# The combining pass beside the last two expert blocks, with their rows made up in two gathered tiles

## The reference, cut to what matters

```python
out = lax.map(expert_block, (blk_expert, buf_tok.reshape(n_blocks, MOE_BLOCK)))
out = out.reshape(n_rows, D_MODEL) * buf_w[:, None]
y = jax.ops.segment_sum(out, buf_tok, num_segments=n_tok + 1)[:n_tok]
...
h = h + hier_moe(...)          # residual
y_prompt = rms_norm(yp, norm_final_w)
y_sample = rms_norm(ys, norm_final_w)
```

## Time and profile before

| | |
|---|---|
| median of 3 runs | 1506.51 us |
| profiled execution's own time | 1505.11 us |
| its span | 1503.4 us |
| PE, DVE, ACT, POOL busy | 1416.1, 1061.5, 766.1, 568.4 us |
| mean rate of the DMA engines | 240 GB/s, 361.07 MB |

### The profile page before, as it was taken

The page is one execution under the profiler, slowest core; times in us unless marked ns, Lnnn a source line. Parts: engine busy times, 40 slices in busy tenths (PEclk is TensorE's granted clock), DMA queues, the critical chain, the costliest instruction groups (busy, mean ns, idle before and its releaser), DMA issues. The chain is left out here.

```text
span 1503.4 us, 21686 instructions
## 1 busy us (share of the span) xinstructions
PE 1416.1 (94%) x7625; PEld 1233.0 (82%) x7625; DVE 1061.5 (71%) x1225; ACT 766.1 (51%) x891; POOL 568.4 (38%) x345
## 2 busy tenths in 40 slices
PE   6999999999999999899999659999999999999976
PEld 5999999999999998788877548888888888888852
DVE  6687722366666664545463579999999999999956
ACT  6332222333333335344433438777777777777734
POOL 2323324454444442485644014333433333333311
PEclk9999999999999999999999669999999999999997
DMA  5222333234444445876653659999999999999958
GB/s 197 65 78 86 126 95 111 80 130 143 144 141 147 138 144 167 294 219 239 209 168 130 231 201 383 402 396 390 377 381 362 389 379 383 385 388 387 369 211 343
DMA packets 115793, 361.07 MB, mean 240 GB/s; under 512 B 18772, under 2 KB 48468, under 8 KB 99348
## 3 DMA queue, kind: packets, MB, share of 16 engines
q1 hardware_dynamic: 100164, 322.37, 58.6%
q0 software_dynamic: 15568, 37.87, 7.3%
HBM read 316.52 MB, written 59.64 MB: 250 GB/s over the span
## 5 line engine op out<-in xcount | busy, mean ns | idle before, releaser
L2048 DVE TENSOR_TENSOR wgu_l<-wgu,wgu_h 128x2048 fp32r<-128x2048 f32 x128 | 290.0, 2288 | 27.4 <-ACT wgu_h L1928 26.5
L1928 ACT CAST wgu_h<-wgu 128x2048 fp32r<-128x2048 f32 x124 | 237.4, 1915 | 100.6 <-PE bank0and L64 100.5
L62 PE MATMUL bank0and<-wgu_h,xh_blk 128*128 128x512 f32 x512 | 203.7, 398 | 2.9 <-DVE xl_blk L2052 2.9
L64 PE MATMUL bank0and<-wgu_h,xl_blk 128*128 128x512 f32 x512 | 200.9, 392 | 0.0
L62 PE MATMUL bank0and<-xh,wh 128*128 128x352 f32 x576 | 197.6, 343 | 3.0 <-ACT raw L906 3.0
L63 PE MATMUL bank0and<-wgu_l,xh_blk 128*128 128x512 f32 x512 | 200.3, 391 | 0.0
L64 PE MATMUL bank0and<-xh,wl 128*128 128x352 f32 x576 | 186.7, 324 | 0.0
L63 PE MATMUL bank0and<-xl,wh 128*128 128x352 f32 x576 | 186.5, 324 | 0.0
L1671 POOL TENSOR_TENSOR wol<-wo,woh 128x1024 fp32r<-128x1024 f32 x48 | 121.4, 2536 | 123.5 <-ACT woh L996 123.5
L1835 POOL DMA_INDIRECT scratch_picked<-yb,dst x31 | 92.7, 2991 | 197.5 <-DVE yb L2042 197.5
L2057 DVE TENSOR_TENSOR wd_l<-wd,wd_h 128x1024 fp32r<-128x1024 f32 x128 | 148.2, 1219 | 1.2 <-ACT wd_h L1934 1.0
(11 more groups left out here) (496 smaller groups left out, 3234.5 us busy)
## 6 DMA issues: line engine op xcount, KB each, us to landing
wgu<-in_w_gate_up SPq DMA_DIRECT2D x128, 1024.0 KB, 7.6
wd<-in_w_down SPq DMA_DIRECT2D x128, 512.0 KB, 7.6
wo<-in_w_out SPq DMA_DIRECT2D x48, 512.0 KB, 4.9
w<-in_w_in_tiles SPq DMA_DIRECT2D x36, 512.0 KB, 3.6
yy<-scratch_picked SPq DMA_DIRECT2D x8, 1024.0 KB, 12.6
scratch_xb<-stage POOLq DMA_DIRECT2D x10, 512.0 KB, 4.0
xb<-scratch_xb SPq DMA_DIRECT2D x8, 640.0 KB, 4.4
scratch_uT<-feat SPq DMA_DIRECT2D x8, 528.0 KB, 5.0
```

The source lines that it names most:

```text
L62: nc.tensor.matmul(acc, lh, rh, start=start, stop=False)
L64: return nc.tensor.matmul(acc, ll, rh, start=False, stop=stop)
L1928: nc.scalar.copy(wgu_h[:, s], wgu[:, s]).then_inc(gu_high, 1)
L2048: nc.vector.tensor_tensor(wgu_l[:, s], wgu[:, s], wgu_h[:, s].bitcast(F32), ALU.subtract).then_inc(gu_split, 1)
```

## The change

`combine` is gone as a function and as a stage; its work is written at the end of each engine's program in `experts`. Order of the parts:

- At the start of `experts` SP writes the gates to DRAM (`gates`, T x 2), and loads `w_final` and the residual tiles 0 to 3 right after the weights of block 1, instead of after the last down load. Residual tiles 8 and 4 now go ahead of the last block's down weights, 5 to 7 behind them.
- POOL zeroes `yb` and scatters it twice, to the rows of `picked` that belong to the last two blocks.
- SP begins to load `yy` when the scatter of block 29 has landed (m*16+32 counts the two extra scatters and blocks 0 to 29) and the part of `wgu_h` that a tile overwrites has been used.
- DVE makes the list `out_row`: the token's number, or out of bounds where one of its two copies is in one of the last two blocks. The output of tiles 0 to 8 goes through indirect stores with this list into one output `y` (T rows).
- POOL scatters blocks 30 and 31 only after every `yy` tile has been loaded, block 31 after block 30 has landed. Then it gathers by the token lists of these two blocks the residual rows, gates and picked rows into two extra tiles, 9 and 10, which are summed, normalised and stored like the others. The store of tile 10 waits for all stores before it.
- PE sums tiles 2, 4, 6, 7; DVE sums 8, 1, 0, 3, 5, 9, 10.

```diff
@@ SP
+            for t in range(2):
+                rows, n = ((slice(0, SEQ), P), (slice(SEQ, T), TS))[t]
+                tiles = slice(0, NT) if t == 0 else slice(NT, NT + 1)
+                sp.dma_start(S["gates"][rows, :].rearrange("(t p) k -> p t k", p=n), S["gate"][0:n, tiles, :]).then_inc(loaded[0], 16)
             m = blocks_but_three(sp) + 1
             load_gate_up(1)
+            sp.wait_ge(rows_ready, 1)
+            sp.dma_start(w_final[:], A["norm_final_w"][0].partition_broadcast(P)).then_inc(loaded[0], 16)
+            for t in range(FIRST):
+                sp.dma_start(h[t], S["h"][t * P:t * P + P, :]).then_inc(loaded[t], 16)
             with sp.Fori(0, m) as i:
                 load_gate_up(i + 2)
                 load_down(i + 1)
+            sp.wait_ge(gu_split, m * 4 + 8)
+            load_h(NT)
+            load_h(4)
             load_down(m + 1)
+            for t in (5, 6, 7):
+                load_h(t)
             sp.wait_ge(y_stored, m * 16 + 32)
+            for t in (8, 1, 0, 2, 3, 4, 5, 6, 7):
+                used = 0 if t == 0 else (t + 1) // 2
+                if used:
+                    sp.wait_ge(gu_used, m * 4 + (4 + used))
+                sp.dma_start(yy[t][0:live(t)], picked[t * P:t * P + live(t)]).then_inc(loaded[t], 16)
@@ POOL
             gather(1)
+            for j in range(2):
+                if j:
+                    pool.wait_ge(y_stored, 16)
+                then_own(pool, nc.gpsimd.tensor_copy(dst[:], of_row[:, 1, bass.ds(m + (1 + j), 1)]), dst_ready, j + 1)
+                pool.indirect_dma_start(out=S["picked"], out_offset=bass.IndirectOffsetOnAxis(ap=dst[:], axis=0),
+                                        in_=yb[:], in_offset=None, bounds_check=2 * T - 1, oob_is_err=False).then_inc(y_stored, 16)
             gather(2)
...
             scatter(m)
+            is_loaded(pool, 0)
+            def store(n):
+                t = ORDER[n]
+                rows = out_row[0:r, t:t + 1] if t <= NT else late_row[:, t - NT - 1, 0:1]
+                pool.wait_ge(out_ready, n + 2)
+                pool.indirect_dma_start(out=A["y"], out_offset=bass.IndirectOffsetOnAxis(ap=rows, axis=0), in_=h[t][0:r, :], ...)
+            late_gather(0, h[NT + 1], S["h"])
+            for j in range(2):
+                late_gather(j, late_gate[:, j, :], S["gates"])
+            for n in range(STORED_FIRST):        # 2
+                store(n)
+            for t in range(NT + 1):
+                is_loaded(pool, t)
             scatter(m + 1)
...                                              # scatter of block 31, after block 30 has landed
+            for n in range(STORED_FIRST, STORED_FIRST + 2):
+                store(n)
+            pool.wait_ge(down_split, m * 4 + 12)
+            pool.wait_ge(y_stored, m * 16 + 80)
+            for k in range(2):
+                late_gather(0, yy[NT + 1][:, k, :], S["picked"], k)
+            late_gather(1, h[NT + 2], S["h"], 0, xg_loaded)
+            for k in range(2):
+                late_gather(1, yy[NT + 2][:, k, :], S["picked"], k, xg_loaded)
+            for n in range(STORED_FIRST + 2, NT + 2):
+                store(n)
+            pool.wait_ge(out_stored, 16 * (NT + 2))
+            store(NT + 2)
@@ DVE, after the loop
+            ...                                  # out_row, four small instructions
+            make_diag(0)
+            make_diag(1)
             gated(m + 1)
             low_down(m + 1, range(2))
             low_hid(m + 1, (last_h, last_l))
+            make_diag(2)
+            make_diag(3)
             unload_y(m)
             low_down(m + 1, range(2, 4))
+            add(NT)
             dve.wait_ge(down_used, (m + 1) * 4 + 4)
             nc.vector.tensor_copy(xg[:], S["banks45"][:]).then_inc(y_done, 1)
+            add(1); norm(NT); add(0); norm(1); norm(0); add(3); norm(2); norm(3); add(5)
+            norm(4); norm(5); norm(6); add(9); norm(7); norm(9)
+            dve.wait_ge(xg_loaded, m * 16 + 80)
+            add(10); norm(10)
```

More of the change, by code:

```diff
@@ L1918, in _ @@
             down(m + 1, first=4)
+            for n, t in enumerate(ON_PE):
+                is_loaded(pe, t)
+                if n == 0:
+                    pe.wait_ge(diag_ready, 8)
+                    pe.wait_ge(hT_done, m + 2)
+                if n >= 2:
+                    pe.wait_ge(y_done, m + (n - 1))
+                for half in range(2):
+                    s = slice(half * 512, (half + 1) * 512)
+                    acc = psum_of(t, half)
+                    nc.tensor.matmul(acc, C["ident"][:], h[t][:, s], start=True, stop=False)
+                    nc.tensor.matmul(acc, diag[n // 2][:, n % 2, 0, :], yy[t][:, 0, s], start=False, stop=False)
+                    nc.tensor.matmul(acc, diag[n // 2][:, n % 2, 1, :], yy[t][:, 1, s], start=False, stop=True).then_inc(pe_summed, 1)
         @block.scalar
@@ L2204, in norm @@
                                                          op0=ALU.mult, op1=ALU.mult)
                 ins.then_inc(out_ready, 1)
[L2207 to L2209 removed]
+            flat_last = in_last[:].rearrange("p t k -> p (t k)")
+            after(nc.vector.tensor_scalar(flat_last, of_block[:], 2.0, blk_end[:, E - 1:E], ALU.add, ALU.is_ge))
@@ new lines, in _ @@
+            after(nc.vector.tensor_reduce(out_row_f[:], in_last[:], AX.X, ALU.max))
+            after(nc.vector.tensor_scalar(out_row_f[:], out_row_f[:], float(4 * T), -1.0, ALU.mult, ALU.add))
+            nc.vector.tensor_tensor(out_row[:], out_row_f[:], C["token_no"][:, :, 0], ALU.add).then_inc(out_ready, 1)
+            make_diag(0)
+            make_diag(1)
+            gated(m + 1)
+            low_down(m + 1, range(2))
+            low_hid(m + 1, (last_h, last_l))
+            dve.wait_ge(hid_ready, m + 2)
@@ L2210, in _ @@
+            make_diag(2)
+            make_diag(3)
+            unload_y(m)
+            low_down(m + 1, range(2, 4))
             add(NT)
+            dve.wait_ge(down_used, (m + 1) * 4 + 4)
+            nc.vector.tensor_copy(xg[:], S["banks45"][:]).then_inc(y_done, 1)
+            add(1)
+            norm(NT)
             add(0)
-            norm(NT)
-            for t in range(2, NT, 2):
-                add(t)
-                norm(t - 2)
-                norm(t - 1)
-            norm(NT - 2)
@@ L2218, in _ @@
-            norm(NT - 1)
+            norm(1)
+            norm(0)
+            add(3)
+            norm(2)
+            norm(3)
+            add(5)
+            norm(4)
+            norm(5)
+            norm(6)
+            add(9)
+            norm(7)
+            norm(9)
+            dve.wait_ge(xg_loaded, m * 16 + 80)
+            dve.sem_inc(holder, 1)
+            add(10)
+            norm(10)
+FIRST = 4
+ON_PE = [2, 4, 6, 7]
+ON_DVE = [8, 1, 0, 3, 5, 9, 10]
+ORDER = [8, 1, 0, 2, 3, 4, 5, 6, 7, 9, 10]
```

220 lines of the change are left out of this document (102 added, 118 removed).

## The result

Slower: 1518.49 us (median of four runs, 1516.45 to 1519.63) against 1506.28 (four runs, 1503.09 to 1506.59), a ratio of 1.0084 with the 95% interval 1.0067 to 1.0102. The prediction had 1503.3 with a range up to 1511. The profiled execution took 1516.45, with a span of 1514.7, where before had 1505.11 and 1503.4. The span grew by 11.3 us; 1.8 less was predicted. So 13.1 us have to be found.

What follows compares the result with a forecast made beforehand. It took the 25.8 us `yy` stream, waiting for two blocks' rows while SP idles, as the bound. Tail to 1501.1 plus 0.5 at the start gave span 1501.6, time 1503.3; own range 1500 to 1506, full range 1497 to 1511.

Steps and rivals of the forecast that it cites:

- first `yy` load issued: SP's start of the stream, after scatter 29 lands and `wgu_h` is used: taken as 1445.5, between 1442.5 and 1447.9.
- from there to the end of the span: End of the kernel: from the end of the last issue to the span's end, 3.75 us as before, giving 1501.1.
- the stream: SP's `yy` loads before the combining pass: 24.5 us long, ending at 1470.0 instead of 1490.4, 20.4 us won.
- POOL's chain: Tail: scatters 30 and 31 after the last `yy` tile, then gathers; 1.6 us per issue while DVE is busy, tile 9 at 1484.7.
- rival A: Tail: POOL keeps up at 1.0 us an issue and DVE's chain sets the end; time 1498.5; chance 0.25.
- Rival B: Tail: DVE's operations hold POOL's indirect issues as in the loop, 2.83 us for 1.6; time 1507.4; chance 0.20.
- DVE's chain: Combining work on DVE: tile 6 done at 1480.7, then 11.2 us of work from add 9 to norm 10.
- no window at clock 0.50: Sign expected in the changed kernel's profile: no window at clock 0.50 before the last matmul.
- The start of the expert blocks: 2.6 MB of extra loads there, mostly hidden: 0.5 us taken, bounds 0 and 6.4.
- rival C: Start of the expert blocks: backlog not hidden, 2.5 or 6.4 us for 0.5; times 1505.3 to 1509.2; chance 0.13.
- `yb` zeroed: Zeroing before the expert blocks, counted as nothing: SP, DMA engines and POOL idle from 864 to 875.
- B with one long hold: Rival B plus one long hold of POOL by DVE, adding 4.5 us: time 1511.9.

Runs made afterwards that it cites:

- one-stage kernel: The kernel before with the combining pass put in the same stage as the experts, nothing else changed: 1506.90 us, ratio 1.0009.
- the two early drains: The changed kernel plus one POOL drain: behind its first two stores, 1515.12 us, ratio 1.0064; or 23 us earlier, 1512.99 us, ratio 1.0050.
- own-array kernel: The changed kernel with the last two blocks written at once to own arrays, those tokens' copies from other blocks left out: 1509.15 us, ratio 1.0025.

## Why the prediction was wrong, step by step

The errors against the prediction's own steps add up to the 13.1 us, but for rounding:

| step | predicted | measured | error |
|---|---|---|---|
| first `yy` load issued | 1445.5 + 0.5 | 1448.18 | +2.2 |
| from there to POOL's release by the last tile | 24.5 | 27.5 | +3.0 |
| from there to tile 9's rows | 14.7 | 16.4 | +1.7 |
| from there to the end of the last issue | 12.6 | 13.0 | +0.4 |
| from there to the end of the span | 3.75 | 9.65 | +5.9 |

**The step that failed is the last one,** in the words on record: "the span at 1503.4, 3.75 later; the same here". I took the distance between two rows for a constant of the program's end. It was 2.6 us of landing, 0.78 of POOL's DRAIN and 0.4 for the rest of the meeting; here it is 2.2 of landing, 7.01 of DRAIN and the same rest. The trace of before had the number for it: 6.49 us of DRAIN at the other meeting, which I had put down as "3.4 us later, after the meeting of all engines". Of a meeting that goes it must be asked what each engine did in it, and where that goes. The one-stage kernel shows it alone (3.1 us won by the missing meeting, 5.2 lost behind the last store), and the two early drains take it away again (4.5 of span in the better one, 5.2 counted from scatter 29). It is not the whole miss: without its 5.9 us the median would be 1512.6, still above the range.

**The second is the stream.** Its start hung on the landing of scatter 29, taken near the middle of 1442.5 to 1447.9; the bound at the deep queue's end was the truth (7.3 us of wait, as the 7.53 in the earlier trace rows): 2.6 MB fewer loads did nothing for it. Its length was to be 1.3 us under that of before, with 1 MB less beside it; it was 1.7 over. By the windows it runs at 391 to 412 GB/s from 1450 to 1472, but begins with 2 us at 150 and ends with 2 us at 272 and a last tile that is late while the engines are already idle. Why the end is ragged was not tried.

**POOL's chain** had the right form and one term at nothing. The issues on its path cost what rival A took, 0.97 to 1.03 us and 0.30 between two, not 1.6, and the writes landed 2.2 us after the end of their issue, for 2.1 predicted. What was left out lies between a release and the indirect DMA behind it: 0.9 us from the copy of the row list to scatter 30, 1.2 from its landing to scatter 31, 0.9 from that one's landing (1484.6) to the next gather, 0.9 from the last norm to the last store. The rows of before had it: DVE's copy ends at 1457.20, the scatter starts at 1458.05, while the plain store at 1499.12 starts 0.3 after its norm. The gather that ends DVE's wait landed after 5.18, not 4.4. So two writes and a gather took 15 us from 1477.00 on, and cheap issues still made a later tile 9.

Rival B, with DVE holding POOL, has a mechanism that is there, but not on this path: between 1477 and 1492 no indirect issue takes over 1.03 us. The trace shows it here as in the earlier trace rows: the three longest issues of the tail (1.34, 1.52 and 1.68 us) end 0.8 to 0.9 us after the end of the DVE operation that they met. Two of them, and these operations:

```profile
1467.20 1.68 POOL L1926 DMA_INDIRECT out_y<-h_first,out_row  x1 [2.77 <-DVE h_first L2253]
1497.18 1.34 POOL L1926 DMA_INDIRECT out_y<-h_rest,out_row  x1 [0.30 <-issue]
```

```profile
1466.71 1.29 DVE L2253 SCALAR_TENSOR_TENSOR h_first<-h_first,st_f,w_final 128x1024 f32<-128x1024 f32 x1
1496.40 1.28 DVE L2253 SCALAR_TENSOR_TENSOR wgu<-wgu,st_f,w_final 128x1024 f32<-128x1024 f32 x1
```

The DVE operations end at 1468.00 and 1497.68, the issues at 1468.88 and 1498.52. An operation lasts 1.3 us here and 2.2 in the earlier trace rows, so an issue loses less. That the operation must read two tiles in SBUF, as the prediction has it, is shown no further than this: all that held an issue in these rows did, and the gather issued at 1457.78 beside DVE's copy out of banks 4 and 5 (start 1457.37, 1.20 us) took 1.06.

**DVE's chain** was right: tile 6 done at 1481.16 for 1480.7 predicted, the 11.2 us from add 9 to the last norm measured as 11.2 (1492.06 to 1503.22). Its wait ahead of add 9 was predicted, at 4.0; it was 10.90, the 4.0 and the three errors ahead of it. The own-array kernel showed that such a wait is worth less than its length, 7.3 us for 10.90, since PE and ACT stand right behind it. The sign "no window at clock 0.50" failed too, without cost: PE waited 2.48 us for its first tile and the mean granted clock was 0.58 from 1460 to 1462, but DVE had other tiles to do.

**The start of the expert blocks** cost 0.6 (DVE's copy for block 29 at 1437.89 against 1437.28), for 0.5 predicted; rival C is out. As the stage began 0.6 us earlier this time (the first DVE rows at 862.49 and 863.10), 1.2 us were lost on the way. But not for the reason given: the DMA engines carried the extra loads at a share of 1.01 from 890 on, where before had 0.74, and PE was no idler:

```profile
890.00:900.00 10.00, 9.13 (x44) 7.44 (x42) 7.01 (x4) 8.02 (x6) 4.11 (x2) 0.99 1.01 410
...
940.00:950.00 10.00, 9.39 (x46) 7.64 (x45) 10.00 (x8) 6.35 (x4) 6.43 (x4) 1.00 1.01 401
```

Most of what was lost lies at 863.5, in a step I had put at nothing, `yb` zeroed:

```profile
863.34 0.96 POOL L1869 MEMSET yb<- 128x1024 f32 x1
863.48 0.86 DVE L2125 TENSOR_SCALAR n_blk<-n_blk 128x32 f32<-128x32 f32 x1
```

The kernel before, without that memset beside it:

```profile
864.08 0.18 DVE L1981 TENSOR_SCALAR n_blk<-n_blk 128x32 f32<-128x32 f32 x1
```

So 0.7 of the 1.2 us went there, on the path to the table of blocks. The rest lies between 883 and 926, where the third gather is issued at 901.83 for 899.38, behind the two scatters of zeros, and the extra loads run; which of them it was stays open. I had listed SP, the DMA engines and POOL as idle, and not asked what DVE did. That the total came out near 0.5 is luck.

**The rivals' sums** have two slips. A leaves out the 0.5 us of the start that the others have (1499.0, not 1498.5), and the range ends at 1511 where B with one long hold gives 1511.9. Neither would have reached the measured time.

## To carry to other kernels

Where stages are merged or an engine's issues are moved between them, find POOL's DRAIN at every meeting in the trace, count the transfers that POOL issued since the one before (0.082 us for each in these kernels), and move that cost along with the work: it should fall where POOL has nothing to do, or the last transfers should be issued by another queue. The distance from the last instruction to the end of the span was 3.75 us in one kernel and 9.65 in the other; take it apart before carrying it over. A transfer by POOL that must have landed before POOL's next step was here a trip of four to five us, however cheap its issue (scatter 30 landed after 3.2 and scatter 31 started 1.2 behind it; the gather landed after 5.18), and the two writes and the gather in a row took 15 us, where the stream had moved ahead by 16.

## What the hardware did that I had not expected

- POOL's DRAIN took 0.082 us for each DMA that POOL issued since its last DRAIN, and some 0.05 more, plain or indirect alike, when all of them had landed: 9 gave 0.784, 10 gave 0.866 and 0.873, 16 gave 1.368, 21 gave 1.762 (twice), 29 gave 2.422, 73 gave 6.028 and 85 gave 7.013. The 6.49 of the first meeting, with 64, holds 1.2 us in which the last scatter was still being issued; from its end it is the count's 5.3. SP's DRAIN took 7 ns to 0.13 us in all these kernels.
- Given while one of POOL's transfers was still under way beside SP's loads (the DMA engines at a share of 0.90, 0.79 and 0.66 during it), it took longer than that count: 8.83 and 9.44 us for 64 transfers, 11.03 for 69 (9.1 from the end of the last issue), where the count gives 5.3 and 5.7. It ended 2.6 to 2.9 us after that transfer had landed in all three (landed at 1448.7, 1449.0 and 1473.9), which speaks for a wait for the landing. At the first meeting of the kernel before, the last scatter lands 3.0 us ahead of the DRAIN's end, so there the count and such a wait can't be told apart. A drain beside such loads with no transfer of POOL's under way was not tried.
- A POOL memset went with a small DVE instruction (TENSOR_SCALAR, 128x32) stretched from 0.18 to 0.86 us, up to the memset's end. Two DVE instructions beside the memset before it kept their 0.46 and 0.45 us.
- An indirect DMA on POOL started 0.9 to 1.2 us after what it had waited for, a plain one 0.3.
- Issuing nine loads took SP 8.07 us when nothing else ran on it, so an engine that only issues was the last at a meeting (1469.8).
